# A hybrid attention and mixture-of-experts block: a branch hint for the back edge of TensorE's loop over the experts

## The reference

```python
h2 = rms_norm(x, norm2_g[l]) * (1.0 + scale2) + shift2
# hierarchical MoE: 4 groups of 8 experts; each token picks one group, then 2 of its 8 experts
for g in range(N_GROUPS):
    a = silu(einsum('bsd,edf->bsef', h, w_gate[g])) * einsum('bsd,edf->bsef', h, w_up[g])
    a = a * comb[:, :, g, :, None]
    out = out + einsum('bsef,efd->bsd', a, w_down[g])
x = x + gate2 * y_moe
```

## Time and profile before

| what | value |
|---|---|
| median of three runs (lowest, highest) | 542.34 us (541.79, 544.69) |
| the profiled execution's own time | 544.22 us |
| its span, from the first to the last instruction | 542.4 us |
| matmuls busy on TensorE (PE) | 502.8 us, 93% |
| weight loads on TensorE (PEld) | 393.7 us, 73% |
| mean granted TensorE clock, share of full speed | 0.975 |
| moved by DMA | 161.89 MB, mean 298 GB/s |

### The profile page before, as it was taken

One profiled execution on the slowest core, in us unless ns is written; L12 is line 12 of the kernel. 1 busy time (PEld: TensorE's weight loads), 2 busy tenths in 40 slices (PEclk: granted clock), 3 DMA queues, 4 the chain that ended last, 5 costly groups with the idle time before them and its releaser, 6 DMA issues.

```text
span 542.4 us, 14805 instructions
## 1 busy us (share of the span) xinstructions
PE 502.8 (93%) x6173; PEld 393.7 (73%) x6174; DVE 186.9 (34%) x567; ACT 150.5 (28%) x281; POOL 153.2 (28%) x195
## 2 busy tenths in 40 slices
PE   4799999999999999999999597999899899899994
PEld 3587888888888888888888475675566556566663
DVE  0631624233423342334213352333233332333333
ACT  3012222223222322232301432232233223223221
POOL 0000010101010101010100005676677667667662
PEclk9799999999999999999999778999999999999999
DMA  8996327394959473725329931979999999999982
GB/s 351 431 434 247 146 77 277 126 429 181 424 213 430 171 284 131 282 88 197 121 106 381 408 112 57 411 266 428 425 434 433 428 431 428 431 430 428 433 350 79
DMA packets 10689, 161.89 MB, mean 298 GB/s; under 512 B 1184, under 2 KB 2464, under 8 KB 3104
## 3 DMA queue, kind: packets, MB, share of 16 engines
q1 hardware_dynamic: 10656, 161.40, 72.5%
HBM read 160.35 MB, written 1.05 MB: 298 GB/s over the span
## 4 chain that ended last, share of the span: by engine, by line
PE 84%; DMA 9%; issue 2%; DVE 2%; ACT 1%; SPq 0%; DVEq 0%; ACTq 0%
PE ps L465 80%; DMA wex<-in_ex 6%; DMA wex<-in_ada 3%; PE ps L710 1%; PE ps L736 1%; ACT act L438 1%; PE ps L711 1%; DVE xT L1032 1%; DVE work L926 0%; PE ps L644 0%; PE ps L643 0%; PE ps L635 0%; PE ps L645 0%; DVE work L967 0%; SPq L279 0%
## 5 line engine op out<-in xcount | busy, mean ns | idle before, releaser
L465 PE MATMUL ps<-act,wmix 128*128 128x256 f32 x864 | 195.0, 382 | 1.0 <-DVE act L816 1.0
L465 PEld LDWEIGHTS ps<-act,wmix 128*128 128x128 f32 x864 | 162.3, 191 | 25.1 <-issue 3.7
L350 POOL TENSOR_SCALAR work<-trig,work 128x256 f32<-128x256 f32 x70 | 65.0, 938 | 71.8 <-issue 62.5
L465 PE MATMUL ps<-wex,work 128*32 128x128 f32 (+1 forms) x1840 | 70.3, 300 | 10.4 <-issue 9.0
L336 POOL TENSOR_TENSOR work<-work,trig 64x256 f32<-64x256 f32 x8 | 5.8, 720 | 252.2 <-ACT work L403 150.6
L465 PE MATMUL ps<-work 32*128 32x256 f32 (+6 forms) x864 | 72.8, 375 | 0.7 <-ACT work L459 0.5
L465 PEld LDWEIGHTS ps<-wex,work 128*32 128x32 f32 x1840 | 50.0, 111 | 28.1 <-issue 13.1
L465 PEld LDWEIGHTS ps<-work 32*128 32x128 f32 (+3 forms) x864 | 47.4, 168 | 13.7 <-issue 3.8
L456 ACT ACT_TABLE_LOAD x35 | 44.9, 1283 | 1.3 <-issue 0.7
L354 POOL TENSOR_TENSOR work<-work,trig 128x512 f32<-128x512 f32 x35 | 44.7, 1278 | 0.0
L465 PE MATMUL ps<-act,work 128*32 128x256 f32 (+1 forms) x704 | 42.2, 360 | 0.9 <-issue 0.9
(11 more groups left out here) (177 smaller groups left out, 433.1 us busy)
## 6 DMA issues: line engine op xcount, KB each, us to landing
wex<-in_ex SPq DMA_DIRECT2D x20, 3072.0 KB, 18.4
wex<-in_ada SPq DMA_DIRECT2D x12, 2048.0 KB, 10.7
wmix<-in_ex SPq DMA_DIRECT2D x8, 3072.0 KB, 19.4
wmix<-in_mix_even SPq DMA_DIRECT2D x4, 3200.0 KB, 10.7
wmix<-in_mix_odd SPq DMA_DIRECT2D x4, 3008.0 KB, 10.7
work<-in_ex SPq DMA_DIRECT2D x4, 2048.0 KB, 19.5
wmix<-in_wo SPq DMA_DIRECT2D x2, 2048.0 KB, 7.3
act<-in_ex SPq DMA_DIRECT2D x4, 1024.0 KB, 14.9
```

What stands on the lines that cost most here:

```text
L350: nc.gpsimd.tensor_scalar(comb_both[:, rows], slot_row[:, rows], lane_now, None, ALU.is_equal).then_inc(comb_half, 1)
L465: return nc.tensor.matmul(out, lhsT, rhs, start=start, stop=stop, **kw)
```

## The change

```diff
             ROUNDS = EXPERTS // EX_SLOTS
-            with pe.Fori(0, ROUNDS) as i:
+            with nc.Fori(0, ROUNDS, engines=[pe.engine], hint_back_edge=True) as i:
                 upto = windows_before(pe, i * EX_SLOTS)
```

## The result

The changed kernel takes 553.44 us (median of 6 runs, 550.37 to 556.8) against 544.78 us for the kernel before beside it (6 runs, 541.79 to 546.15): 1.0165 times, 95% interval 1.0116 to 1.0213. It is slower by some 9 us, where no change that can be measured was forecast. The profiled execution took 553.0 us, with a span of 551.2 us instead of 542.4.

What follows compares the result with a forecast made beforehand. TensorE's sequencer was taken as the bound, weight transfers nearly level. Four hints add 0.4 us and the back edges 0: 542.34 + 0.4 = 542.7 us for the median, range 541.6 to 544.0 us.

Steps and rivals of the forecast that it cites:

- What bounds the kernel: Experts' loop: TensorE's sequencer and weight transfers nearly level; TensorE's losses reach the end in full, gains at most 0.3 us.
- The back edge: Outer loop's three taken branches: target already in instruction memory, so the hint saves 0, with -0.45 us kept as a bound.
- Rivals A and B: Outer back edge: A, hint cheapens taken branch, 542.3 or 542.0 us, chance 0.17; B, hides unseen fetch, 542.0 us, chance 0.03.
- The instruction itself: Head of each trip: one added hint of about 0.1 us, four times, +0.4 us (bounds 0 and 1.5 us).
- The sum: Whole kernel: profiled 544.22 + 0.4 + 0 = 544.6 us; for the median 542.34 + 0.4 = 542.7 us.
- all is resident after the first trip ... I cost this at 0: TensorE's code behind the hint: moved by one instruction's length against the fetched blocks' borders, costed at 0.
- rival C: Loop body: hint fetches though the target is held and drives out needed code, 545.7 to 563.7 us, chance 0.12.
- the two signs named for rival C: Loop: packets of q8 in the later trips, and gaps named "issue" amid a window, would show C (chance 0.12).

Runs made afterwards that it cites:

- place 138: Kernel before with the loop's first instruction laid at place 138 of a block of 256: 1.0433 times without the hint, 546.78 us (1.0057 times) with it at the head.
- the late hint: Hint armed just ahead of the outer branch, against the kernel before: 543.69 us, 1.001 times; the same with the loop at place 138 of a block: 1.0399 times.
- the fourth trip without one: Written-out loop with the hint armed at the head of trips one to three only, against the kernel before: 546.84 us, 1.0057 times.
- the long body: Two trips of fourteen window copies instead of four of seven, against the kernel before: 564.0 us (1.0386 times) without the hint, 569.86 us (1.0502 times) with it.

## Why the prediction was wrong

*What bounds the kernel* held. TensorE's sequencer sets the end, and a loss in it goes through in full: the stall of 4.5 us behind the loop reached the end, with 2.7 us of slower work behind it on top.

*The back edge* held. The body stays in the engine's memory, the taken branch costs 0.22 us though its target is there, and the hint took nothing off it. Rivals A and B are out: 236 ns, and gaps of 1.52 to 1.54 us.

*The instruction itself* was under-sized. From the first matmul of the second trip to that of the third were 424.45 - 382.97 = 41.48 us before; the changed kernel has

```profile
381.71 1.52 issue
383.23 2.82 PE ps L465 x80
...
423.50 1.54 issue
425.04 2.82 PE ps L465 x80
```

41.81 us, 0.33 more; the next trip has 0.48 more (41.84 against 41.36). The sum had 0.1 for a trip. The gap at the head takes 0.1 to 0.2 of it. Another 0.1 lies at the ends of the inner loops, whose branches mostly show 82 or 87 ns in these trips where they had 67. The rest is open. The plain instruction in the hint's place made a trip only 0.1 us longer, which is what the sum had for the hint. What slows the inner branches is open too. With the hint ahead of the seventh copy, the seventh's branch shows 80 ns and the others 67 or 72, as if it were the armed hint; but with the hint just ahead of the outer branch all show 78 (line 760 there). The trips of that kernel are 0.2 to 0.3 us longer than before, which its time (1.001 times) can't tell from nothing. The inner loops' line of the changed kernel, and of that one:

```profile
L755 PEldq COMPARE_BRANCH  x30: 70/82/261, 333.7 to 506.2; - x30
...
L760 PEldq COMPARE_BRANCH  x30: 73/78/233, 333.8 to 504.1; - x30
```

*The step that failed* is "all is resident after the first trip ... I cost this at 0", with the parts of the prediction that took the hint's effect to be confined to the back edge. I read the seven packets of the first trip as the body's own code. A trip of 1,693 instructions is 6.6 blocks of 256; beside the head's block six are enough, and the seventh belonged to the code behind the loop. I had asked what the hint might fetch too much (rival C) and not what it might keep from being fetched. It neither fetched nor drove out anything: the target was held, and the request that it replaced was the one for the next code in line. Of the two signs named for rival C one did come, a gap called "issue" amid a window, but behind the loop and without a packet in the later trips. The price of a request that is missing, a fetch of 6.2 us from question to use of which 4.5 showed as a stall, stands in no row of before.

The Trainium skill has the sizes right and its warning doesn't apply as it stands. "Runtime: NRT & Kernel Launch", section "Instruction fetch mechanics", gives TensorE 2,048 instructions in blocks of 256: eight blocks, which agrees with place 138, where eight stay and the ninth costs some 24 us. The same section's window of two pages would make every back edge here a miss; the branch of 221 ns and three trips without a packet contradict it.

Which block a packet carries isn't in the trace. That the missing one is the block behind the loop follows from the counts, from the place of the stall, which is the same with 37 matmuls in three executions and moves with the code as counted above, and from the runs that bring the packet back: the late hint and the fourth trip without one. When the next block is asked for is inferred: the sharper form is the simplest that fits these runs, except in one place. Open is why the second back edge at place 138 without a hint took 0.24 us, with no packet for the block behind, and the third 6.3 (with the late hint it is the same), and why a block costs small gaps in the long body. For the latter a fetch of 6.2 us is about as long as a block takes to run (241 instructions in 5.8 us); that is argued, not tested.

None of the kernels is measurably faster than the one before.

## What to carry to other kernels

Before hinting a back edge, look at whether code is fetched in the later trips at all, and at how long the taken branch is: with no packets and 0.22 us there is nothing to win. Then count the body in blocks and ask which request the hint displaces; if the loop is left soon and code follows it, that code is the next thing to be missing: here a fetch of 6.2 us, of which 4.5 showed, plus 2 to 3 us of slower work behind the stall. The hint paid where the loop fitted exactly and the request for one block more drove its head out (some 20 us here). Where the back edge did miss and the branch stood far into its block, it took 4.8 us off the one back edge and lost 4.4 us at the exit. With many back edges for each exit it might pay there, which no run shows.

## What the runs showed of the hardware that I had not expected

- A request for code takes 6.2 us from question to first instruction, though its packet takes 1 us; two in a row 6.3 to 7.4 us.
- The head's place within a block decides between 543 and some 567 us (the ratio of 1.0433) for the same instructions: a body of 6.6 blocks can touch seven or eight.
- The hinted target isn't asked for when the hint is armed, 99 us ahead, but, as far as the two distances tell, at the entry into the branch's block: 67 instructions of lead hid 1.2 us, 220 hid 4.8 us.
- Untaken branches of the inner loops take 67 ns as a rule without a hint and up to 87 ns with one; whether the hint is armed at the time doesn't settle it.
